# Opening of a two-block kernel: modulation columns by pairs on TensorE, features and first products chunk by chunk, and the root of the norm on four columns

## What is computed

```python
def rms_norm(x):
    xf = x.astype(jnp.float32)
    return (xf * lax.rsqrt(jnp.mean(xf * xf, axis=-1, keepdims=True) + EPS)).astype(x.dtype)

def modulate(x, shift, scale):
    return rms_norm(x) * (1.0 + scale) + shift

s_lat = jax.nn.silu(c)[:, None, :]
s_ctx = jax.nn.silu(c_ctx)[None, None, :]
mod_l = jnp.split(s_lat @ ada_w[i] + ada_b[i], ADA_CHUNKS, axis=-1)
mod_c = jnp.split(s_ctx @ ada_w[i] + ada_b[i], ADA_CHUNKS, axis=-1)
h_lat = modulate(x_lat, mod_l[0], mod_l[1])
h_ctx = modulate(x_ctx, mod_c[0], mod_c[1])
```

## Time and profile before

| what | us |
|---|---|
| median of 3 runs (lowest, highest) | 3100.14 (3099.31, 3103.01) |
| span of the profiled execution, first to last instruction | 3093.0 |
| PE busy in the span | 2980.1 (96%) |
| DVE busy | 2090.1 (68%) |
| ACT busy | 1189.8 (38%) |
| POOL busy | 178.9 (6%) |

### The profile page before, as it was taken

One profiled execution on the slowest core, in us unless ns is written; L12 is line 12 of the kernel. 1 busy time (PEld: TensorE's weight loads), 2 busy tenths in 40 slices (PEclk: granted clock), 3 DMA queues, 4 the chain that ended last, 5 costly groups with the idle time before them and its releaser, 6 DMA issues.

```text
span 3093.0 us, 41680 instructions
## 1 busy us (share of the span) xinstructions
PE 2980.1 (96%) x15064; PEld 2470.7 (80%) x15064; DVE 2090.1 (68%) x3193; ACT 1189.8 (38%) x1806; POOL 178.9 (6%) x148
## 2 busy tenths in 40 slices
PE   7999999999999999998999999999999999999898
PEld 5787678888877799875888888788878878986897
DVE  6963588877786756787798886556655632645755
ACT  3223434332243654544342323442334422422553
POOL 1300000000001000000030210000000000001120
PEclk9999999999999999999999999999999999999999
DMA  7662054666623156310256562673256622542554
GB/s 272 203 218 93 31 183 163 213 204 238 204 97 106 55 184 226 121 55 28 82 187 214 166 195 67 215 234 101 97 197 222 221 87 91 163 166 87 186 188 144
DMA packets 125376, 479.83 MB, mean 155 GB/s; under 512 B 13768, under 2 KB 13768, under 8 KB 122912
## 3 DMA queue, kind: packets, MB, share of 16 engines
q1 hardware_dynamic: 119232, 443.60, 43.4%
q0 software_dynamic: 5984, 34.04, 3.0%
HBM read 459.76 MB, written 17.83 MB: 154 GB/s over the span
## 4 chain that ended last, share of the span: by engine, by line
PE 69%; DVE 13%; issue 12%; ACT 3%; DMA 2%; SPq 1%; POOL 0%; DVEq 0%; ACTq 0%; PEldq 0%; POOLq 0%
PE bank L757 20%; PE bank L759 20%; PE bank L758 20%; PE bank L1612 2%; ACT w_hi L1679 1%; PE bank L1013 1%; DVE w_lo L2360 1%; DVE tmp L3324 1%; DVE ada_junk_a L2371 1%; ACT tmp L1679 1%; DMA ada_first<-in_ada 0%; DMA ml_v<-v_spill 0%; DVE x_res L2462 0%; PE bank L1384 0%; PE bank L1586 0%
## 5 line engine op out<-in xcount | busy, mean ns | idle before, releaser
L2360 DVE TENSOR_TENSOR w_lo<-w_raw,w_hi 128x1024 fp32r<-128x1024 f32 x617 | 752.8, 1228 | 598.5 <-ACT w_hi L1679 581.0
L1679 ACT ACTIVATE w_hi<-w_raw 128x1024 fp32r<-128x1024 f32 x620 | 649.1, 1054 | 726.6 <-PE bank L759 705.3
L757 PE MATMUL bank<-h_hi,w_hi 128*128 128x512 f32 (+1 forms) x2008 | 699.1, 348 | 36.9 <-DVE h_lo L2436 9.4
L758 PE MATMUL bank<-h_lo,w_hi 128*128 128x512 f32 (+1 forms) x2008 | 692.0, 345 | 0.0
L759 PE MATMUL bank<-h_hi,w_lo 128*128 128x512 f32 (+1 forms) x2008 | 691.4, 344 | 0.0
L757 PEld LDWEIGHTS bank<-h_hi,w_hi 128*128 128x128 f32 x2008 | 385.6, 192 | 89.8 <-issue 32.1
L758 PEld LDWEIGHTS bank<-h_lo,w_hi 128*128 128x128 f32 x2008 | 385.6, 192 | 45.3 <-issue 1.2
L759 PEld LDWEIGHTS bank<-h_hi,w_lo 128*128 128x128 f32 x2008 | 385.3, 192 | 43.9
L757 PE MATMUL bank<-w_hi,xm_hi 128*128 128x512 f32 x512 | 201.7, 394 | 0.0
L759 PE MATMUL bank<-w_hi,xm_lo 128*128 128x512 f32 x512 | 200.3, 391 | 0.0
L758 PE MATMUL bank<-w_lo,xm_hi 128*128 128x512 f32 x512 | 200.2, 391 | 0.0
(11 more groups left out here) (448 smaller groups left out, 5045.7 us busy)
## 6 DMA issues: line engine op xcount, KB each, us to landing
w_raw<-in_weights SPq DMA_DIRECT2D x620, 512.0 KB, 3.6
ada_ring_f<-in_ada SPq DMA_DIRECT2D x56, 512.0 KB, 3.4
ada_ring_g<-in_ada SPq DMA_DIRECT2D x44, 512.0 KB, 3.7
ada_ring_b<-in_ada SPq DMA_DIRECT2D x38, 512.0 KB, 4.1
ada_ring_a<-in_ada SPq DMA_DIRECT2D x32, 512.0 KB, 3.4
ada_first<-in_ada SPq DMA_DIRECT2D x16, 512.0 KB, 15.3
v_spill<-ml_v POOLq DMA_DIRECT2D x4, 1024.0 KB, 5.0
o_spill<-ml_o_grp POOLq DMA_DIRECT2D x4, 1024.0 KB, 4.6
```

Source lines behind the costliest of these rows:

```text
L757: mm(out, lhs[0], rhs[0], start=start, stop=False)
L758: mm(out, lhs[0], rhs[1], start=False, stop=False)
L1679: return nc.scalar.activation(out, in_, func, **kw)
L2360: V.tensor_tensor(WLO[:, slot, :], RAW[:, slot, :], WHI[:, slot, :].bitcast(F32), SUB)\
```

## The change

The SP queue loads `x` first, in four parts, then the ada tiles as pairs of shift c and scale 8 + c. PE makes all eight shifts and scales 8 and 9; DVE makes scales 10 to 15. Squares are summed in pairs of chunks by DVE, and PE multiplies them as the stationary operand by one column of ones, so that the sum of a token lies on its partition (128 x 4 in all); root and reciprocal are taken there, ACT scales four copies of the identity, and PE multiplies them by ones, which gives the reciprocal root in every partition of bank 7. DVE multiplies `x` by it once per chunk. Pairs 0 and 1 are multiplied before the first chunk's products; pair c + 1 (from chunk 3 on; 2 and 3 ahead of chunk 2) ahead of the products of chunk c. `turn_over` is new: matmuls of 256 columns in bank 2 whose result nobody reads. ACT adds the shift itself (scale and bias), then copies to `h_hi`. Renamed semaphores (`SHARED` and the `N(...)` of their later waits) shift counts only and are left out here.

```diff
-ADA_TENSOR = (3, 5, 7, 9, 11, 13, 15)
+ADA_PAIRS = [(c, DC + c) for c in range(DC)]
+ADA_TENSOR = tuple(range(DC + 2))
+X_PARTS = 4
@@ SP
-            sp.dma_start(C_ROWS[:, 0:2, :], c_rows_d[:, 0:2, :]).then_inc(S("c_rows_in"), 16)
-            for n in range(ADA_FIRST):
-                sp.dma_start(ADA_RAW[:, n, :], ada[n]).then_inc(S(f"ada_first{n // 2}"), 16)
-                if n == 5:
-                    sp.dma_start(X[:, :, :], x_t).then_inc(S("x_first"), 16)
-                if n == 9:
+            for part in range(X_PARTS):
+                sp.dma_start(X[:, 2 * part:2 * part + 2, :], x_t[:, 2 * part:2 * part + 2, :])\
+                    .then_inc(S(f"x_first{part}"), 16)
+            for p, pair in enumerate(ADA_PAIRS):
+                for n in pair:
+                    sp.dma_start(ADA_RAW[:, n, :], ada[n]).then_inc(S(f"ada_first{p}"), 16)
+                if p == 1:
                     for s in range(LOOKAHEAD):
                         sp.dma_start(RAW[:, s, :], weights[s]).then_inc(raw_full[s], 16)
+                    sp.dma_start(C_ROWS[:, 0:2, :], c_rows_d[:, 0:2, :]).then_inc(S("c_rows_in"), 16)
@@ POOL
-            for n in range(LOOKAHEAD):
+            for n in range(LOOKAHEAD - 1):
...
+            pool.wait_ge(S("ada_pe_done"), DC - 1)
             pool.dma_start(ROPE[:, :, :, :], ret_rope_d).then_inc(S("vecs_in"), 16)
@@ PE
-            pe.wait_ge(S("silu_c_done"), 1)
-            for i, n in enumerate(ADA_TENSOR):
...
-            pe.wait_ge(S("std_done"), 1)
-            gemm_rows("ret_qk", TOK, 0, ["qk_free"], 16)
+            def turn_over(n):
+                for _ in range(n):
+                    mm(PS[2][:, 0:256], MOD[:, 96:224], MOD[:, 128:384], start=True, stop=True)
+
+            pe.wait_ge(S("mod_zero"), 1)
+            turn_over(6)
+            pe.wait_ge(S("consts_in"), 32)
+            for part in range(X_PARTS):
+                if part:
+                    turn_over(1)
+                pe.wait_ge(S("sq_pair"), part + 1)
+                for b in range(4):
+                    last = mm(PS[6][:, b:b + 1], XSQ[:, 2 * part, b * P:(b + 1) * P], ONES[:, 0:1],
+                              start=part == 0 and b == 0, stop=part == X_PARTS - 1 and b == 3)
+            last.then_inc(S("sq_used"), DC)
+
+            def ada_pair(p):
+                if p == 0:
+                    pe.wait_ge(S("silu_c_done"), 1)
+                pe.wait_ge(S(f"ada_first{p}"), 16 * 2)
+                for i, n in enumerate(n for n in ADA_PAIRS[p] if n in ADA_TENSOR):
+                    for k in range(DC):
+                        last = mm(PS[3 + p % 3][:, 2 * i:2 * i + 2], ADA_RAW[:, n, k * P:(k + 1) * P],
+                                  vec("c_cols", 2 * k, 2), start=k == 0, stop=k == DC - 1)
+                    if p < 2:
+                        turn_over(1)
+                last.then_inc(S("ada_pe_done"), 1)
+
+            for b in range(4):
+                pe.wait_ge(S("rstd_diag"), b + 1)
+                last = mm(PS[7][:, b * P:(b + 1) * P], ONES[:, :], tmp(2)[:, b * P:(b + 1) * P], start=True, stop=True)
+            last.then_inc(S("rstd_rows"), 1)
+            ada_pair(0)
+            ada_pair(1)
+            turn_over(3)
+
+            def first_pairs(k):
+                for p in {2: (2, 3)}.get(k, (k + 1,) if 3 <= k < DC - 1 else ()):
+                    ada_pair(p)
+            gemm_rows("ret_qk", TOK, 0, ["qk_free"], 16,
+                      before=first_pairs)
@@ ACT
+            f(CELL[:, 1:2], vec("eps"), ACT.Sqrt)
+            for part in range(X_PARTS):
+                act.wait_ge(S(f"x_first{part}"), 16)
+                f(XSQ[:, 2 * part:2 * part + 2, :], X[:, 2 * part:2 * part + 2, :], ACT.Square)\
+                    .then_inc(S("sq_done"), 2)
+            act.wait_ge(S("sq_used"), DC)
+            f(STD4, PS[6][:, 0:4], ACT.Sqrt, scale=1.0 / D, bias=vec("eps", 0)).then_inc(S("std_done"), 1)
+            act.wait_ge(S("consts_in"), 32)
+            act.wait_ge(S("rstd_cols"), 1)
+            for b in range(4):
+                f(tmp(2)[:, b * P:(b + 1) * P], IDENT[:, :], ACT.Copy, scale=RSTD4[:, b:b + 1])\
+                    .then_inc(S("rstd_diag"), 1)
             for n in range(LOOKAHEAD):
                 hi(n, n, first=True)
-            h_hi(0, TOK, shifts(0, 0))
+            for c in range(DC):
+                act.wait_ge(S("xn_done"), c + 1)
+                act.wait_ge(S("ada_pair"), 2 * c + 2)
+                if c >= 4:
+                    act.wait_ge(S("h_lo_done"), c - 3)
+                for st, cols in STREAMS:
+                    last = f(hbuf(c)[:, cols], XN[:, c, cols], ACT.Identity, scale=mod(0, 1, c, st),
+                             bias=mod(0, 0, c, st))
+                last.then_inc(S("raw_done"), 1)
+                act.wait_ge(S("raw_done"), c + 1)
+                f(HHI[:, c, :], hbuf(c), ACT.Copy).then_inc(S("h_hi_done"), 1)
+                if c == 1:
+                    act.wait_ge(S("c_rows_in"), 16)
+                    f(C_ROWS[:, 0:2, :], C_ROWS[:, 0:2, :], ACT.Silu).then_inc(S("silu_c_done"), 1)
@@ DVE
+            V.memset(MOD[:, 96:384], 0.0).then_inc(S("mod_zero"), 1)
+            for part in range(X_PARTS):
+                a, b = (XSQ[:, 2 * part + i, :] for i in range(2))
+                dve.wait_ge(S("sq_done"), 2 * part + 2)
+                V.tensor_tensor(a, a, b, ADD).then_inc(S("sq_pair"), 1)
+            dve.wait_ge(S("std_done"), 1)
+            V.reciprocal(RSTD4, STD4).then_inc(S("rstd_cols"), 1)
+            dve.wait_ge(S("vecs_in"), 16)
+            dve.wait_ge(S("rstd_rows"), 1)
+
+            def x_normed(c):
+                dve.wait_ge(S(f"x_first{c // 2}"), 16)
+                V.tensor_tensor(XN[:, c, :], X[:, c, :], PS[7][:, :], MUL).then_inc(S("xn_done"), 1)
+
+            def first_mods(p):
+                shift, scale = (MOD[:, 2 * n:2 * n + 2] for n in ADA_PAIRS[p])
+                b_shift, b_scale = (vec("ada_b", n) for n in ADA_PAIRS[p])
+                if p >= 2:
+                    dve.wait_ge(S("silu_c_done"), 2)
+                    dve.wait_ge(S(f"ada_first{p}"), 16 * 2)
+                    own(ada_product(DC + p, ADA_RAW[:, DC + p, :], AREA_A))
+                    V.tensor_scalar(scale, scale, b_scale, 1.0, ADD, ADD).then_inc(S("ada_pair"), 1)
+                dve.wait_ge(S("ada_pe_done"), p + 1)
+                V.tensor_scalar(shift, PS[3 + p % 3][:, 0:2], b_shift, None, ADD).then_inc(S("ada_pair"), 1)
+                if p < 2:
+                    V.tensor_scalar(scale, PS[3 + p][:, 2:4], b_scale, 1.0, ADD, ADD).then_inc(S("ada_pair"), 1)
+
+            def first_lo(c):
+                dve.wait_ge(S("h_hi_done"), c + 1)
+                V.tensor_tensor(HLO[:, c, :], hbuf(c), HHI[:, c, :].bitcast(F32), SUB).then_inc(S("h_lo_done"), 1)
+
+            for c in range(4):
+                x_normed(c)
+            first_mods(0)
+            for c in range(4, DC):
+                x_normed(c)
+            dve.wait_ge(S("w_lo_done"), LOOKAHEAD - 1)
+            lo(LOOKAHEAD - 1, LOOKAHEAD - 1)
+            first_lo(0)
+            first_mods(1)
+            first_lo(1)
+            first_mods(2)
+            for p in range(3, DC):
+                first_mods(p)
+                first_lo(p - 1)
+            first_lo(DC - 1)
```

More of the change, by code:

```diff
@@ L131 @@
           "lat_sq": ("rg_free", 24),
-          "lat_used": ("ada_pe_done", 1),
+          "lat_used": ("ada_pe_done", DC),
           "lat_std": ("ada_first0", 32),
@@ L181 @@
           "xcl_back": ("diff_tab_in", 32),
-          "x_back": ("x_first", 16),
+          "x_back": ("x_first0", 16),
           "rows_read": ("lam_dot", 1),
+          "hn_tr": ("x_first1", 16),
+          "ml_cols": ("x_first2", 16),
+          "rows_done": ("x_first3", 16),
+          "hn_done": ("mod_zero", 1),
+          "ml_den": ("sq_pair", 4),
+          "ml_num": ("rstd_diag", 4),
+          "ml_arg": ("rstd_cols", 1),
+          "ml_exp": ("xn_done", 8),
+          "rb_mm": ("ada_pair", 16),
+          "rb_copy": ("rstd_rows", 1),
           "q_done_act": ("lam_exp", 1)}
@@ L242, in program @@
         ADA_RAW = at("ada_first", [P, ADA_FIRST, 1024], ARENA)
+        XSQ = at("x_squares", [P, DC, TOK], H_AT)
+        XN = at("x_normed", [P, DC, TOK], H_AT + 16 * K)
+        STD4, RSTD4 = FUSE[:, 0:4], FUSE[:, 4:8]
         QK = at("ret_qk_sb", [P, 16, TOK], ARENA)
@@ L724, in _ @@
             pool.dma_start(MV2[:, :, :], v_spill).then_inc(S("v_back"), 16)
-            pool.wait_ge(S("rb_copy"), 8)
+            pool.wait_ge(S("rb_copy"), N("rb_copy", 8))
             for g in range(2):
@@ L864, in ln_between, with gemm_rows @@
                         ctx_square_sum(q, i)
-            def gemm_rows(ph, T, m, free, body=8, granted=0, upd0=None, half=None, ahead=LOOKAHEAD):
+            def gemm_rows(ph, T, m, free, body=8, granted=0, upd0=None, half=None, ahead=LOOKAHEAD,
+                          before=None):
                 g0, kinds = FIRST[ph], len(free)
```

(26 more changed lines are left out.)

18 lines of the change are left out of this document (6 added, 12 removed).

## The result

The changed kernel takes 3116.03 us (median of 4 runs, 3109.80 to 3118.04) against 3099.72 (4 runs, 3098.51 to 3103.01) in the same comparison: ratio 1.0053, 95% interval 1.004 to 1.0065. It is 16.3 us slower. The forecast was 3119, and faster, same and slower had 0.11, 0.18 and 0.71.

A forecast was written before the change was run, and what follows sets the result against it. PE, busy 96% of the span, was taken as the bound: tile 3 at 85.7 instead of 66.7 adds 19.0 to the 3093.0 span, 3112.0, plus 7.1 gives 3119 us; likeliest case 3112 to 3129, full range 3097 to 3130.

The forecast's parts named there:

- Narrow work ahead of the first chunk at the slow level: PE's sums, root and rows, pairs 0 and 1 and turn_over at slow pace: first chunk at 44.3, not 29.1.
- The silu of `c_rows` as DVE's gate, and chunk 2: DVE's six products wait behind ACT's silu, which ends at 46.9; chunk 2 on PE starts at 54.5.
- The middle between slow and fast steps: PE's four steps, chunk 2 to chunk 6: 6.6 us each, between 4.9 fast and 8.35 slow; chunk 6 at 80.9.
- The last two chunks: Chunks 6 and 7 on PE follow each other, mostly fast, 4.8 us, ending at 85.7.
- Rival D: Chunk steps on PE: every group starts and ends slow, each step 8.35, time 3129; chance 0.10.
- The reference point: Start of tile 3 in the kernel before, taken as 66.7; the opening's gain or loss is counted from it.
- From span to time: Whole program: 7.1 us, the median's distance above the profiled span, added to the forecast span of 3112.0.
- The sum of 19.0: Opening up to tile 3: 85.7 - 66.7 = +19.0 us, added to the profiled span of 3093.0.
- B: Opening: turn_over keeps PE at 2.4 GHz throughout; first chunk at 29.1, -2.3 us, 3098; chance 0.15.
- C: Opening and chunks: as B, but DVE paces the chunks, steps of 3.47; -6.9 us, 3093; chance 0.10.
- C's condition, the hidden wait: Chunk steps: if PE's wait for h_lo of chunk c behind tile c + 1 is hidden, a step falls to 3.5.

The follow-up runs named there:

- e2: The change with DVE making the low part of chunk c before it waits for PE's tile c + 1: 3105.95 us, ratio 1.0034 to the kernel before.
- e11: As e10, but PE makes only the eight shifts, DVE all eight scales, shifts 0 to 3 ahead of the first chunk: 3087.51 us, ratio 0.9965 to before.
- e10: The change without turn_over, silu of c_rows early, low part before the wait, one tile ahead of each of chunks 1 to 6: 3100.07 us, ratio 1.0004.
- e3: The change with two more turn_over, in bank 6, behind each of the six tiles between the chunks: 3110.99 us, ratio 1.0044 to the kernel before.
- e7: The kernel before with only squares summed in pairs, root and reciprocal on four columns, and PE's broadcast: 3097.26 us, ratio 0.9995.
- e9_root_split_warm: As e7, with ada tile 15 moved from PE to DVE and four turn_over in PE's gap before the first chunk: 3096.23 us, ratio 0.9987 to before.
- e5_silu_early: The change with ACT's silu of c_rows ahead of the first chunk instead of behind the second: 3113.59 us, ratio 1.0054 to the kernel before.
- e8_before_warm: The kernel before with five turn_over in PE's gap between the last ada tile and the first chunk: 3096.41 us, ratio 0.9989.
- e1_no_turn: The change without any of its turn_over matmuls: 3108.30 us, ratio 1.0034 to the kernel before.
- e4_pairs_first: The change with all pair tiles ahead of the first chunk and the eight chunks without a break behind them: 3113.73 us, ratio 1.0047 to before.

## Why the prediction was right, and where it was off

*Narrow work ahead of the first chunk at the slow level:* right. The tiles and their fourth `turn_over` ended at about 40.8 for 41.7, and the first chunk started at 43.1 for 44.3. The difference is the start: `vecs` landed at 7.8 and not 8.4, and root and rows took 2.9 and not 3.2.

*The silu of `c_rows` as DVE's gate, and chunk 2:* right. DVE's first product began at 45.5 (46.9 forecast), chunk 2 at 54.1 (54.5). The working let pair 1 be done at 41.7, with the `turn_over` behind it; its signal comes from the tile's last matmul, ahead of that `turn_over`, and DVE read it at 40.1.

*The middle between slow and fast steps:* right in kind, low in size. It was a choice between two bounds and not worked out, so that 6.6 came near 7.0 is in part luck. The four steps came to 28.0 us, 7.0 on average, for 6.6; the clock fell and rose four times between 52.6 and 86.7. The last two chunks, which I had called mostly fast, took 5.9 for 4.8. Chunk 6 started at 82.1 (80.9 forecast) and tile 3 at 88.0 (85.7). The wait for `h_lo` was 0.91, where I had 1.1 for it and the handovers.

In the trace the chunks at 54.1 and 62.4 start slow, with the clock already down since 52.6; those at 69.1, 75.6 and 82.1 start fast, and the clock falls 0.5, 0.9 and 1.2 us into them. The Trainium skill (TensorE: Matmul & The Clock Gate, "HAM oscillation — how this bites in real kernels") describes groups of matmuls parted by waits that each start at the low clock; the waits there are for DMAs, of 3 to 5 us each. The trace shows the same kind of alternation with waits of only 0.91, beside two-column matmuls, but not that every group starts slow. Rival D, every step at 8.35, did not come: one step in four (8.3) was like that.

*The reference point:* wrong by 1.2. I took tile 3's start in the kernel before as 66.7, from the end of DVE's wait for tile 0. But tiles 0, 1 and 2 end one after the other, and the six matmuls of the other two came behind. Tile 3 started at 67.9. So the opening lost 20.1 and not 21.3, for a forecast of 19.0; with 67.9 in its sum the forecast would have been 17.8.

*From span to time:* wrong. I set 7.1 us around the span, the distance of the median from one profiled span. The runs show 1.8 (3115.9 and 3117.7 in the same execution). The other 5 us were that the profiled execution of the kernel before was one of its quicker ones. The sum of 19.0 was then made against a quick execution, and the median moved by 16.3. Behind tile 3 the changed kernel's profiled execution also took 2.8 us more, which the sum did not have. So the 3119 against 3116 is better than the working: 5.3 us of the 7.1 answered to nothing in the change, and they made up for the 1.1 us by which the opening was forecast too short and for these 2.8. That it came within 3 us is in part luck; the direction and the mechanism are not.

*Rivals.* B and C needed 2.4 GHz throughout the narrow work. In the change the clock was at 0.50 from 8.2 to 45.7, and in no run with its ten `turn_over` there was it back before 42.6 (e2). C's condition, the hidden wait, is what e2 makes true, and its step was 3.9 (PE's own work) and not DVE's 3.5. That the order of loads would be the limit never came up: neither PE nor DVE waited for an ada tile in the changed kernel.

## What to carry to other kernels

Before matmuls of few columns are put between wide ones, price them at the clock they will run at and the clock they leave behind: the same tile cost 3.41 or 1.79 us here, and nine wide matmuls 3.84 or 2.04. The runs point to two things: that wide matmuls follow each other before narrow ones come between them (e11 against e10), and that PE does not wait between groups (e2, e3). One instruction moved ahead of a wait on another engine (e2) made tile 3 start 11.9 us earlier. An engine that has idle time early should take narrow work from the engine that sets the end: here DVE, whose first product began at 45.5 in the change and at 26.4 in e11.

## What was unexpected

Added work on the busiest engine made the opening shorter (e3), by filling 0.9 us gaps.

The rest of the program is not constant. From tile 3 to the end the profiled spans leave 3021 to 3029 us, and this goes with how long the clock stood at 1.2 GHz after 100 us, added up from the clock records of each trace (each sum takes in some 2 us behind the last instruction):

| kernel | from tile 3 to the end, us | at 1.2 GHz after 100 us |
|---|---|---|
| e9_root_split_warm | 3021.3 | 65.3 |
| e7_root_alone | 3021.7 | 72.5 |
| e5_silu_early | 3024.0 | 75.2 |
| e11_shifts_only | 3024.4 | 78.4 |
| e2_lo_first | 3026.2 | 81.9 |
| the change | 3027.9 | 82.1 |
| before | 3025.1 | 82.3 |
| e8_before_warm | 3025.9 | 82.4 |
| e1_no_turn | 3026.7 | 85.3 |
| e10_mended | 3026.3 | 85.4 |
| e3_hold | 3027.0 | 85.5 |
| e4_pairs_first | 3028.9 | 85.5 |

The instructions behind tile 3 are the same in all of them. So a change of a few microseconds in the opening is better read at the start of tile 3 than in the median: e7 lost 2.4 us there and its median did not show it. Whether a shift of the opening itself moves those later stretches, or chance does, is not settled by one profile of each.
